# Hybrid attention layer with mixture of experts: x is also loaded transposed, and 1/rms is applied when projection sums are read

## What the reference computes

```python
h = rms_norm(x, g_mix)                    # x is 256 tokens x 1024
proj = h @ w_in + b_in                    # gq gk gv gr g_lr sq sk sv gate_a gate_b
y_a = gla(gq, gk, gv, decay(g_lr), gr) @ w_gla_out      # gated linear attention, 4 heads
y_b = swa_with_sinks(rope(sq), rope(sk), sv) @ w_swa_out  # window of 128, 16 query heads
mixed = sigmoid(gate_a) * y_a + sigmoid(gate_b) * y_b
x = x + mixed @ w_out
x = x + moe_ffn(rms_norm(x, g_ffn))       # 32 experts, top 4, clamped SwiGLU
return rms_norm(x, g_final)
```

## Time and profile before

| | |
|---|---|
| median of 3 runs | 1194.38 us (1194.31 to 1195.21) |
| profiled execution | 1193.74 us, span in the trace 1191.9 us |
| busy in the span | PE 96%, DVE 36%, ACT 22%, POOL 12% |
| DMA | 376 GB/s over the span |
| granted TensorE clock | 0.997 of full speed on average |

### The profile page before, as it was taken

One profiled execution on the slowest core, in us unless ns is written; L12 is line 12 of the kernel. 1 busy time (PEld: TensorE's weight loads), 2 busy tenths in 40 slices (PEclk: granted clock), 3 DMA queues, 4 the chain that ended last, 5 costly groups with the idle time before them and its releaser, 6 DMA issues.

```text
span 1191.9 us, 17974 instructions
## 1 busy us (share of the span) xinstructions
PE 1139.2 (96%) x7389; PEld 553.3 (46%) x7389; DVE 423.3 (36%) x817; ACT 256.7 (22%) x442; POOL 141.8 (12%) x103
## 2 busy tenths in 40 slices
PE   7999999999999999999999999999999999999996
PEld 5988999984333333333333333333333333333332
DVE  6988744854222222222222222222222222222223
ACT  5465746332111111111111111111111111111112
POOL 5545543561000000000000000000000000000000
PEclk9999999999999999999999999999999999999999
DMA  7634336789999999999999999999999999999995
GB/s 283 248 145 158 111 138 251 292 317 368 426 427 428 428 427 433 429 433 429 434 434 429 434 428 435 429 433 429 433 431 432 431 432 432 432 426 427 430 427 233
DMA packets 27331, 447.68 MB, mean 376 GB/s; under 512 B 3216, under 2 KB 3344, under 8 KB 5632
## 3 DMA queue, kind: packets, MB, share of 16 engines
q1 hardware_dynamic: 26640, 446.05, 89.2%
q0 software_dynamic: 224, 0.71, 0.2%
q10 hardware_dynamic: 432, 0.42, 0.1%
HBM read 446.12 MB, written 1.05 MB: 375 GB/s over the span
## 4 chain that ended last, share of the span: by engine, by line
PE 55%; DMA 37%; DVE 6%; issue 1%; ACT 1%; DVEq 0%; SPq 0%
DMA ring<-wexp 36%; PE PS L896 31%; PE PS L623 12%; PE PS L889 3%; PE PS L881 2%; PE PS L913 1%; PE PS L672 1%; PE PS L748 1%; DMA EXT<-be 1%; DVE slot_R L1269 1%; PE PS L722 1%; DVE EXT L1307 1%; DVE SQ L1721 0%; DVE SQ L1724 0%; PE PS L735 0%
## 5 line engine op out<-in xcount | busy, mean ns | idle before, releaser
L896 PE MATMUL PS<-ring,SQ 128*64 128x512 f32 x1536 | 350.1, 597 | 20.5 <-DMA ring<-wexp 19.2
L896 PE MATMUL PS<-ring,PTG 128*64 128x512 f32 x1024 | 240.2, 600 | 10.3 <-DMA ring<-wexp 10.2
L896 PEld LDWEIGHTS PS<-ring,SQ 128*64 128x64 f32 x1536 | 103.7, 136 | 233.2 <-issue 199.0
L1216 ACT ACTIVATE SQ<-SQ 128x256 f32<-128x256 f32 x64 | 26.7, 417 | 600.0 <-DVE SQ L1717 600.0
L547 POOL TENSOR_TENSOR slot_R<-ring,slot_R 128x512 fp32r<-128x512 f32 (+1 forms) x76 | 117.8, 1581 | 99.9 <-ACT slot_R L1013 99.9
L896 PEld LDWEIGHTS PS<-ring,PTG 128*64 128x64 f32 x1024 | 66.5, 136 | 132.2 <-issue 129.9
L896 PE MATMUL PS<-EXT,SQ 128*64 128x512 f32 x512 | 116.9, 598 | 0.9 <-DMA EXT<-wexp 0.2
L1717 DVE TENSOR_SCALAR SQ<-PS 128x256 f32<-128x256 f32 x64 | 27.2, 425 | 243.2 <-PE PS L896 243.2
L623 PE MATMUL PS<-slot_R 128*128 128x256 f32 (+2 forms) x288 | 90.1, 313 | 0.0
L1013 ACT ACTIVATE slot_R<-ring 128x2048 fp32r<-128x2048 f32 (+1 forms) x38 | 70.8, 1869 | 39.1 <-DMA ring<-wblk 22.0
L889 PE MATMUL PS<-PTG,BRW 64*128 64x512 f32 x264 | 74.2, 640 | 0.8 <-DVE PTG L1736 0.8
(11 more groups left out here) (277 smaller groups left out, 1143.4 us busy)
## 6 DMA issues: line engine op xcount, KB each, us to landing
ring<-wexp SPq DMA_DIRECT2D x50, 4096.0 KB, 30.1
ring<-wexp SPq DMA_DIRECT2D x59, 2048.0 KB, 19.2
EXT<-wexp SPq DMA_DIRECT2D x10, 4096.0 KB, 39.6
ring<-wblk SPq DMA_DIRECT2D x36, 1024.0 KB, 4.8
EXT<-wexp SPq DMA_DIRECT2D x12, 2048.0 KB, 20.5
ring<-wexp SPq DMA_DIRECT2D x2, 1024.0 KB, 33.4
BRW<-brow SPq DMA_DIRECT2D x7, 256.0 KB, 6.0
ring<-wskv SPq DMA_DIRECT2D x2, 544.0 KB, 9.3
```

Source lines behind the costliest of these rows:

```text
L896: last = mm(PS[g * SLOTS:(g + 1) * SLOTS, b, :], lhsT, rhs[:, g * 512:(g + 1) * 512], start=start, stop=stop)
L1216: fn(SGM[:, part], GLU[:, part], ACT.Sigmoid, scale=ALPHA).then_inc(sgm_ready, 1)
```

## The change

The host also lays out x transposed (`xt`, 128 x 2048), and SP loads it in two halves around the first weight unit, which comes in two pieces. x itself comes after unit 2. High and low parts of x * g_mix are made from `xt` without r (`high_x` on ACT, `low_x` on DVE, straight from SBUF). The first block is multiplied by pairs of k, and the low parts of units 0 and 1 are made half by DVE, half by POOL. The 16 transposes go; the scales' four matmuls move behind quarter (0,1) of block 1. Token-major sums are now read as sum * r + bias in the same instruction. Feature-major sums are read by DVE with a multiplication by `RSR`, and ACT adds the bias (or takes the sigmoid) in place in SBUF afterwards. `RSR` now lies at the end of the ring, so that SP's second early expert chunk waits until sum 25 has been read.

```diff
@@ SP
-            for i in range(TT):
-                sp.dma_start(X[:, i, :], x[i * P:(i + 1) * P, :]).then_inc((x_in, x_in1)[i], 16)
+                if c == 1:
+                    evacuated(sp, GATES_DONE - 1)
+                if u == 0:
+                    x_columns(0)
+                    half = unit_width(0) // 2
+                    sp.dma_start(w_unit(0)[:, 0:half], wblk[0, :, 0:half]).then_inc(unit_in[w_slot(0)], 16)
+                    sp.dma_start(w_unit(0)[:, half:2 * half], wblk[0, :, half:2 * half]).then_inc(first_in, 16)
+                    x_columns(1)
+                if u == 2:
+                    for i in range(TT):
+                        sp.dma_start(X[:, i, :], x[i * P:(i + 1) * P, :]).then_inc((x_in, x_in1)[i], 16)
+                    bias(0)
+                if u == 3:
+                    bias(1)
+                    sp.dma_start(TAB[:, T_SWA:NTAB], tab[:, T_SWA:NTAB]).then_inc(tab_in, 16)
@@ POOL
+            for u in range(2):
+                pool.wait_ge(hi_ready, u + 1)
+                half = unit_width(u) // 2
+                nc.gpsimd.tensor_tensor(w_unit(u, True)[:, half:2 * half], w_unit(u)[:, half:2 * half],
+                                        h_unit(u, True)[:, half:2 * half].bitcast(F32), ALU.subtract).then_inc(lo_p, 1)
@@ TensorE
+                for u in range(2):
+                    for k0 in range(0, KH, 2):
+                        n = 2 * u + k0 // 2
+                        pe.wait_ge(ht_hi, n + 1)
...
+                        product(u, 0, 0, k0)
+                        product(u, 0, 0, k0 + 1)
+                        pe.wait_ge(ht_ready, n + 1)
+                        product(u, 1, 0, k0)
+                        product(u, 1, 0, k0 + 1)
...
+            def scales_across():
...
-            dense(1)
+            dense(1, {(0, 1): [scales_across]})
@@ ACT
+            for u in range(2):
+                high_x(2 * u)
+                first_split(u, 0)
+                high_x(2 * u + 1)
+                first_split(u, 1)
+            split(2)
             for i in range(TT):
                 act.wait_ge((x_in, x_in1)[i], 16)
                 fn(SQ[:, i, :], X[:, i, :], ACT.Square, accum_out=S_SS[:, i:i + 1]).then_inc(ssq0, 1)
@@ ACT feature_major
-                    act.wait_ge(pj_full[u % NPJ], u // NPJ + 1)
+                    evacuated(act, 2 * i + half)
                     for f in range(2):
+                        part = dst[half][:, f * SEQ:(f + 1) * SEQ]
+                        last = fn(part, part, func, bias=col(c + 2 * half + f))
-                    last.then_inc(pj_free[u % NPJ], 1)
+                    last.then_inc(gates_done, 1)
@@ ACT
-            feature_major(4, [GKT[:, c * BW:(c + 1) * BW] for c in range(2)], C_BK, ACT.Identity)
             for a in range(2):
                 act.wait_ge(qt_full, a + 1)
                 fn(qT[:, 2 * a:2 * a + 2, :], PS[:, 4 + a, :].rearrange("p (k t) -> p k t", k=2), ACT.Copy).then_inc(qt_cp, 1)
+            feature_major(4, [GKT[:, c * BW:(c + 1) * BW] for c in range(2)], C_BK, ACT.Identity)
@@ DVE
+            for u in range(2):
+                low_x(2 * u)
+                low_x(2 * u + 1)
+                first_rest(u)
+            rest(2)
             mean_eps(S_SS, S_VAR, D, ssq0, TT, var0)
...
             rest(3)
+            def feature_major(u, dst):
+                dve.wait_ge(pj_full[u % NPJ], u // NPJ + 1)
+                v.tensor_tensor(dst.rearrange("p (f t) -> p f t", f=2), bk(u % NPJ).rearrange("p (f t) -> p f t", f=2),
+                                RSR.unsqueeze(1).broadcast_to([P, 2, SEQ]), ALU.mult).then_inc(pj_free[u % NPJ], 1)
                 if u == 3:
+                    dve.wait_ge(rsr_full, 1)
+                    link(v.tensor_copy(RSR, PS[:, 3, 0:SEQ]))
                     rotate_queries(0)
             v.scalar_tensor_tensor(W0, TMP, -1.0, TMP, ALU.mult, ALU.min).then_inc(gate_neg, 1)
+            for half in range(2):
+                feature_major(6 + half, GQT[:, half * BW:(half + 1) * BW])
             rest(10)
...
                 v.tensor_copy(qT[:, 2 * a:2 * a + 2, :], PS[:, 4 + a, :].rearrange("p (k t) -> p k t", k=2)).then_inc(qt_ready, 1)
+            for half in range(2):
+                feature_major(8 + half, GKT[:, half * BW:(half + 1) * BW])
@@ DVE, after the loop of window attention
+            dve.wait_ge(gr_ready, 3)
+            for half in range(2):
+                feature_major(18 + half, MIX[half])
             rest_t(OB2, obt_full, obt_lo)
             rest(24)
+            for half in range(2):
+                feature_major(20 + half, MIX[2 + half])
...
+            feature_major(22, GB[0])
             rest(26)
+            feature_major(23, GB[1])
             rest(28)
+            feature_major(24, GB[2])
             rest_t(OA2, oat_full, oat_lo)
+            feature_major(25, GB[3])
```

More of the change, by code:

```diff
@@ L138, in tables, with program @@
     return t
[L141 removed]
+def program(nc, x, xt, wblk, wskv, wgate, cv, rows, brow, tab, wrout, be1, be2, gfin, wexp, out):
     with ExitStack() as ctx:
@@ L196, in program @@
         LRT = in_tail(SEQ)
+        RSR = in_tail(SEQ)
         ident = TAB[:, T_ID:T_ID + P]
@@ L577, in _ @@
             mm = nc.tensor.matmul
[L580 to L589, removed]
-                    for i in range(TT):
-                        last = mm(PS[:, 3, i * P:(i + 1) * P], TAB[:, T_ONE:T_ONE + P], DIAG[:, i * P:(i + 1) * P],
-                                  start=True, stop=True)
-                    last.then_inc(rsr_full, 1)
             usage = [0]
@@ L678, in _ @@
+            def scales_across():
+                pe.wait_ge(diag_ready, TT)
+                for i in range(TT):
+                    last = mm(PS[:, 3, i * P:(i + 1) * P], TAB[:, T_ONE:T_ONE + P], DIAG[:, i * P:(i + 1) * P],
+                              start=True, stop=True)
+                last.then_inc(rsr_full, 1)
             first_block()
-            dense(1)
+            dense(1, {(0, 1): [scales_across]})
             dense(2)
@@ L1025, in _, with first_split, high_x @@
             preload(ACT.Sqrt)
+            def first_split(u, part):
+                width = unit_width(u) // 2
+                c = slice(part * width, (part + 1) * width)
+                if u == 0 and part:
+                    act.wait_ge(first_in, 16)
+                else:
+                    landed(act, u)
+                fn(h_unit(u, True)[:, c], w_unit(u)[:, c], ACT.Copy).then_inc(hi_ready if part else first_hi, 1)
+            def high_x(n):
+                act.wait_ge(xt_in[n // 2], 16)
+                for k in range(2 * n, 2 * n + 2):
+                    last = fn(HT_R[:, k, :], HTL[:, k, :], ACT.Copy, scale=col(C_GMIX + k))
+                last.then_inc(ht_hi, 1)
+            act.wait_ge(ident_in, 16)
+            preload(ACT.Sqrt)
+            act.wait_ge(cv_in, 16)
+            for u in range(2):
[4 more added lines that the diff above has]
+            split(2)
             for i in range(TT):
@@ L1030, in _ @@
             fn(S_SD, S_VAR, ACT.Sqrt).then_inc(sd0, 1)
-            split(0)
-            for a in range(4):
-                act.wait_ge(ht_raw, 2 * (a + 1))
-                fn(HT_R[:, 2 * a:2 * a + 2, :], HTL[:, 2 * a:2 * a + 2, :], ACT.Copy).then_inc(ht_hi, 1)
-                if a == 1:
-                    split(1)
-            for u in range(2, 10):
+            for u in range(3, 10):
                 split(u)
@@ L1403, in decay_products @@
                 if level == 0:
-                    for u in range(6, 10):
-                        evacuated(dve, u)
+                    dve.wait_ge(gates_done, 4)
                     dve.wait_ge(decay_out, 1)
```

107 lines of the change are left out of this document (45 added, 62 removed).

## The result

The changed kernel takes **1207.59 us** (median of 4 runs, 1206.28 to 1208.34). The kernel before took 1194.8 beside it (4 runs, 1194.31 to 1196.08). The ratio is 1.0112, with a 95% interval of 1.0095 to 1.0128: slower by 12.8 us, where +11.0 was predicted. The profiled execution took 1208.34 us with a span of 1206.5, which is 14.6 more than the span before. It is the slowest of the four, so its rows add up to somewhat more than the median shows.

The account below looks back on a forecast made before the run. Before 260 us TensorE's progress was taken to set the total, with the order on DVE deciding. Terms 0 + 0.5 + 2.0 + 3.6 + 1.5 + 2.6 + 1.7 - 0.9 = +11.0 us gave 1205.4 us, range 1198 to 1210.

Parts of the forecast that it names:

- the test: Sign that the forecast is right: block 10 starts at 156.5 us; reached before 152 us, it is wrong.
- Sum 6: Block 4's quarter (0,1): DVE reads gq's sum behind `gate_neg`, at 60.3 us where 58.3 is needed; +2.0 us (1.5 to 2.5).
- Sum 8: Block 5's (0,1): gk's read comes late through ACT's gq passes, uncovered table load and DVE's list; +3.6 us (2.5 to 4.5).
- Sum 18: Block 10's (0,1): DVE reads ga0's sum only after `rest(22)`, at 154.2 us; +2.6 us (2 to 3).
- The clock: Rival, chance 0.1: clock falls to half in the pause at sum 8, +1.5 us, as much again at sum 18; 1208.
- The start: Blocks 0 and 1: earlier block 0, but the lead is lost at DVE's read of sum 0; 0, within 0.7 either way.
- the copy of RSR: Between sum 3 and `rotate_queries(0)` in DVE's full stretch, delaying the read of sum 4; +0.5 us (0 to 0.6).
- POOL against DVE: Attention's first slots: POOL's low part of unit 13, begun later, slows DVE's `block_exponents`; +1.5 us (0 to 2.5).
- Block 13: Sums 22 to 25: TensorE waits for `rest_t(OA2)`, ending at 199.3 us where 197.7 is wanted; +1.7 us (0.6 to 2.4).
- Biases: Block 14: the biases' transfer comes earlier for TensorE, which had waited 0.87 us behind it; -0.9 us (-0.9 to 0).
- SP's new wait: Wait for sum 25 holds an expert chunk and unit 31 by some 2 us; free, as unit 31's buffer frees later.
- The loop: Expert loop's stream is started by TensorE's progress, so every microsecond gained or lost before 260 us counts in the total.

Follow-up runs that it names:

- the start alone: Changed kernel, but ACT reads feature-major sums from PSUM in the old places, 1/rms left out of gq, gk and both gates: 1198.0 us, ratio 1.0026.
- the reads alone: Kernel before, with feature-major sums read by DVE, multiplied by ones, in the changed kernel's places, and ACT adding the bias in place: 1207.06 us, ratio 1.0103.
- Exp first: Changed kernel, with ACT computing Exp and Ln of the gate before the bias pass over gq: 1202.7 us, ratio 1.0079.

## Why the prediction was right

**The time and its direction.** 1205.4 was said, within 1198 to 1210; 1207.59 was measured, also inside the forecast's own range of 1202 to 1208. Block 10 starts at 156.26, where 156.5 was said as the test. The three large waits were right in place, cause and size. That the total came so near is in part luck: up to 4.8 us of clock that the sum left out stand against terms that were too high by 2.3, and the profiled run, which has all of the 4.8, is the slowest of the four. The "eight reads" of the first paragraph are twelve, as a later one says; no term hangs on the count.

**Sum 6**: predicted +2.0; the wait was 1.7 and the lag grew by 2.0. The read stands behind `gate_neg` as said and ends near 60.3.

**Sum 8**: predicted +3.6; the wait was 3.6. Exp was put at 62.95 and came at 63.42, the read at 77.4 and it came at 77.1 to 77.8. That the chain runs through ACT's passes and the uncovered table load was shown by the edit that moves only these passes.

**Sum 18**: predicted +2.6; the wait was 2.4, behind `rest(22)` as said. Moving the read alone brought 4.7 us back.

**The clock** was a rival at 0.1 with +1.5 at each of sums 8 and 18, and was kept out of the sum. In the profiled execution it happened besides the waits, at just these places and for +1.6 each, and for about 1.6 more than before in the router, which the sum had not listed. These 4.8, and 0.9 for the biases, less 1.4 of POOL's term, 0.6 of block 13's and 0.3 at the start and the copy, lead from 11.0 to the 14.4 of the table. The chance was too low: the prediction took one quiet trace as evidence against it, though that trace had no pause over 0.8 us behind the first to try it on.

**The start**: term 0, and it was mis-sized, in the steps as well as in the sum. Block 0 started at 9.32 instead of 8.0, since ACT's first instruction had waited for TAB until 6.85, and the roundings of x and of half a unit follow it. From there to block 1's start it took 12.5 us instead of 11.7; four passes of `low_x` took 6.04 us beside POOL in it. With these the lead at block 1 was 1.7 where 4 was said. Unit 3 landed at 21.3 and not at 20.0. ACT rounded it from 21.55, after the square root that waited for DVE, and DVE read sum 0 at 25.7 instead of 24.2 to 24.9. The wait in block 1 was shorter than said (1.8 for 2.6) only because TensorE came later to it. The experiment with the start alone gives the term its price: +3.1 us at the end (1.1 to 5.3), of which 1.3 by the first scores, 0.6 of them at sum 4, where the copy of RSR was predicted at +0.5. The +0.2 of the table is one of two outcomes of the same instructions. Eight traces share this start, and the mark at 47.6 us stands 0.1 to 0.4 us behind the kernel before in three of them, and 1.2 to 1.4 in five; in those five TensorE waits 1.3 us at sum 4 instead of 0.3. In those five one more of DVE's passes in `rotate_queries(0)` took 1.66 us beside POOL instead of 0.69.

**POOL against DVE**: predicted +1.5, measured 0.1 in the changed kernel and 1.2 when the pause that covered it was gone. The mistake was to add up two delays of which the one gives the other time to pass.

**Block 13**: predicted +1.7; +1.1, and the wait is for the end of `rest_t(OA2)`, as said.

**Biases**: predicted -0.9; 0. The wait at L1629 is still 0.6 us. The transfer did come earlier for TensorE: it landed at 217.01 us against 205.64, 11.4 later, where TensorE was 12.8 later. But DVE's first two passes over the biases now fell beside POOL's next unit (busy from 213.80 to 219.83) and took 3.3 us instead of 1.9, and the 1.4 us were gone. What was missed is that collision, and not the transfer.

**SP's new wait**: said to be free. TensorE has no wait on a transfer between the start and 300 us.

**The loop**: named as the step with the least proof. The expert loop has the same pace in both traces, and the lag of 14.4 us ahead of it is 14.6 at the end of the span. In every experiment's trace, with lags from 0.7 to 14.7 us at 300 us, the lengthening of the span is within 1 us of that lag. It held.

By the ratios the reads alone cost 12.3 us, the start alone 3.1 and both together 13.4, with about 2 us either way on each. So the two parts may simply add up, or the start may cost less with the reads behind it; these runs don't tell.

## What to carry to other kernels

Before an operation moves to an engine that is 36% busy, look at what is queued ahead of it in its place: a read of 0.64 us cost 1.7 to 3.6 us of waiting here, because it stood behind a pass that nobody waited for, and again through a third engine whose table load lost its cover. Work taken off the busiest engine pays only if the next buffer, the next read and the next transfer are early too; here the start's lead of 1.7 us was gone 5 us later. Count the clock beside each new pause of TensorE as long as these: it fell behind about half of them, for 1.5 us and more. And when a wait is mended, expect what lay beneath it: most of the single edits brought out another one.

## What the runs showed of the hardware

Pauses of TensorE can be followed by a stretch at the 1.2 GHz level, in some executions and not in others. The traces of the changed kernel and of the experiments, by pause (a fall shows in the granted clock of the windows; the last column is what the lag grew by beyond the wait):

| pause | traces | clock fell in | lag beyond the wait, us |
|---|---|---|---|
| sum 6, 1.6 to 1.8 us | 6 | 2 | 1.8 with a fall, 0.3 without |
| sum 8, 3.6 us | 3 | 3 | 1.6, 2.7, 3.0 |
| sum 18, 2.4 to 2.7 us | 6 | 4 | 1.7 to 1.8 with a fall, 0.3 without |
| block 14, 2.3 to 2.4 us | 3 | 2 | 1.8 with a fall, 0.3 without |
| the attention's transposes (L754), 1.1 to 1.9 us | 5 | 1 (the 1.9) | 3.7 with the fall |

So a fall mostly cost 1.5 us, and at two places up to 2.7 and 3.7. Between block 0 and the router the clock fell nowhere in these traces without such a pause ahead of it. Its length alone doesn't decide it: at sum 18 the clock fell behind 2.4 us with Exp first, and stayed up behind 2.7 us with `split(13)` moved as well:

```profile
156.00:166.00 10.00, 8.09 (x56) 8.09 (x57) 4.12 (x6) 6.49 (x10) 4.52 (x4) 0.83 0.23 82
...
156.00:166.00 10.00, 8.09 (x69) 8.09 (x70) 5.52 (x8) 7.39 (x10) 4.52 (x4) 1.00 0.28 106
```

Beside POOL (busy from 11.00 to 17.3 us) `low_x` took 1.51 us (four in 6.04), and 0.44 ahead of it. Other DVE instructions that were slowed there lost about as much, whatever their size: the 2048 columns of `rest` took 3.2 us instead of 2.3, 512 columns with both inputs in SBUF 1.66 to 1.82 instead of 0.69, an operation on four columns 1.23 instead of 0.17. That is 0.9 to 1.1 us each, so small operations pay relatively most. The new reads, with one operand in PSUM, took the same 0.68 us beside POOL (at 207.31).

Not every instruction with both inputs in SBUF paid. The subtraction of 1024 columns kept its 1.2 us at 10.81, as at 17.91 without POOL. It had begun 0.2 us ahead of POOL's own subtraction, and that one took 3.28 us where POOL's next of the same shape took 2.42. So here POOL seems to have been the one that lost; one case doesn't prove a rule:

```profile
10.00 0.88 DVE L1311 SCALAR_TENSOR_TENSOR slot_R<-ring,CV,HT_R 128x256 fp32r<-128x256 f32 x2 [0.77 <-ACT HT_R L1059]
10.81 1.22 DVE L1319 TENSOR_TENSOR slot_R<-ring,slot_R 128x1024 fp32r<-128x1024 f32 x1
11.00 3.28 POOL L539 TENSOR_TENSOR slot_R<-ring,slot_R 128x1024 fp32r<-128x1024 f32 x1 [8.88 <-ACT slot_R L1053]
...
17.91 1.21 DVE L1319 TENSOR_TENSOR slot_R<-ring,slot_R 128x1024 fp32r<-128x1024 f32 x1
```
